# A diffusion backbone on one core: the first layer's modulation weights loaded by the features they make

## The reference, cut to what matters

```python
sh1, sc1, g1, sh2, sc2, g2 = split(silu(cvec) @ w_ada[l] + b_ada[l], 6)   # w_ada[l]: 1024 x 6144
hm = rmsnorm(x, norm_pre_mix[l]) * (1 + sc1) + sh1                        # modulate
rq, rk, rv, ... = split(hm @ w_in[l])                                     # first product
```

## Time and profile before

| | before |
|---|---|
| median of 3 runs | 2224.93 us (2220.21 to 2231.7) |
| the profiled execution, its own time | 2224.93 us |
| its span, first to last instruction | 2223.2 us |
| mean granted TensorE clock | 0.987 |
| TensorE busy | 2139.6 us, 96% |
| VectorE, ScalarE, GpSimd busy | 1562.2, 927.7, 112.7 us |

### The profile page before, as it was taken

How to read it: one execution, slowest core, us unless ns; L and a number is a source line. 1 busy time by engine, 2 the same in 40 slices (tenths; PEclk the granted TensorE clock), 3 DMA queues, 4 the chain that set the end, 5 groups by cost and what they waited for, 6 DMA issues and landing times. The chain is left out here.

```text
span 2223.2 us, 34106 instructions
## 1 busy us (share of the span) xinstructions
PE 2139.6 (96%) x14080; PEld 2029.8 (91%) x14080; DVE 1562.2 (70%) x2451; ACT 927.7 (42%) x1462; POOL 112.7 (5%) x208
## 2 busy tenths in 40 slices
PE   5999999999998999999979999999999989999997
PEld 3999999999978899999869999999999888999996
DVE  5677766477757787887776776755764557787785
ACT  4644432466243433333365454325653433333332
POOL 1000000110000000000000000111100000000000
PEclk9999999999999999999989999999999999999998
DMA  7333244234344222222323332542233411222223
GB/s 278 118 108 111 91 166 141 100 99 149 101 133 158 67 77 87 85 77 95 142 109 114 114 114 82 171 148 78 89 115 70 178 57 58 95 76 81 91 76 133
DMA packets 62955, 246.22 MB, mean 111 GB/s; under 512 B 8080, under 2 KB 8112, under 8 KB 60240
## 3 DMA queue, kind: packets, MB, share of 16 engines
q1 hardware_dynamic: 41040, 153.12, 20.9%
q0 software_dynamic: 21760, 90.91, 11.7%
HBM read 230.34 MB, written 13.66 MB: 110 GB/s over the span
## 5 line engine op out<-in xcount | busy, mean ns | idle before, releaser
L1499 DVE TENSOR_TENSOR wl<-raw,wh 128x1024 fp32r<-128x1024 f32 x204 | 247.1, 1222 | 148.7 <-ACT wh L1080 145.9
L476 PE MATMUL unit<-hmh,wh 128*128 128x320 f32 x1152 | 348.1, 310 | 2.9 <-DVE sig L1978 2.6
L477 PE MATMUL unit<-hml,wh 128*128 128x320 f32 x1152 | 347.4, 309 | 0.0
L1080 ACT ACTIVATE wh<-raw 128x1024 fp32r<-128x1024 f32 x204 | 210.0, 1050 | 128.1 <-DMA raw<-w_main 128.1
L479 PE MATMUL unit<-hmh,wl 128*128 128x320 f32 x1152 | 263.1, 310 | 0.0
L1599 DVE CUSTOM_DVE_ANT_0 junk<-ada,csb,par 128x1024 f32<-128x1024 f32 x160 | 205.6, 1285 | 29.1 <-DMA ada<-w_ada 9.0
L476 PEld LDWEIGHTS unit<-hmh,wh 128*128 128x128 f32 x1152 | 216.9, 188 | 4.1 <-issue 3.4
L477 PEld LDWEIGHTS unit<-hml,wh 128*128 128x128 f32 x1152 | 216.9, 188 | 0.7
L464 PE MATMUL unit<-wh,hmh 128*128 128x256 f32 (+1 forms) x640 | 201.6, 315 | 9.5 <-DVE t L1525 3.6
L466 PE MATMUL unit<-wh,hml 128*128 128x256 f32 (+1 forms) x640 | 199.8, 312 | 0.0
L465 PE MATMUL unit<-wl,hmh 128*128 128x256 f32 (+1 forms) x640 | 199.6, 312 | 0.0
(11 more groups left out here) (435 smaller groups left out, 5257.9 us busy)
## 6 DMA issues: line engine op xcount, KB each, us to landing
raw<-w_main SPq DMA_DIRECT2D x276, 512.0 KB, 4.1
ada<-w_ada POOLq DMA_DIRECT2D x80, 512.0 KB, 4.3
first<-w_first SPq DMA_DIRECT2D x8, 1024.0 KB, 19.3
x<-x_keep POOLq DMA_DIRECT2D x3, 2560.0 KB, 9.5
bias<-biases POOLq DMA_DIRECT2D x32, 192.0 KB, 2.7
x<-x POOLq DMA_DIRECT2D x2, 2560.0 KB, 12.4
x_keep<-x POOLq DMA_DIRECT2D x10, 512.0 KB, 2.9
bias<-biases POOLq DMA_DIRECT2D x16, 256.0 KB, 4.1
```

The costliest lines, as they stand in the source:

```text
L476: pe.matmul(u[:, h, 0:n], a[0], xs[h][0], start=f, stop=False)
L477: pe.matmul(u[:, h, 0:n], a[0], xs[h][1], start=False, stop=False)
L1080: act.activation(wh[slot[i]][:, :], raw[slot[i]][:, :], ACT.Copy).then_inc(w_hi[slot[i]], 1)
L1499: dve.tensor_tensor(wl[slot[i]][:, :], raw[slot[i]][:, :], f32(wh[slot[i]][:, :]), ALU.subtract)\
```

## The change

The first modulation weights are cut the other way: piece c now holds all 1024 input features of the 2 x 128 outputs (shift and scale) that modulate chunk c. TensorE's sums of one piece are 8 matmuls of 256 columns in four column groups (`first_sums`). The sums lie in rows 0 and 1 of each group of 32 rows, and one matmul with two columns of `zpos` (ones at the rows that are 0 or 1 modulo 32) both adds the four groups and turns them to columns (`turn_rows`). So that the other rows are zero, `cc` is padded to 32 columns. VectorE makes one chunk's shift and scale, modulates the chunk, and so on. On TensorE sums, turns and the products of the first two columns are interleaved in one loop. The tokens are loaded first, in three parts, on SyncE's queue; slabs 0 and 1 go ahead of piece 3. `x_back` counts one less, as the tokens have semaphores of their own.

```diff
-        zpos = fixed("zpos", [P, 2])
+        zpos = fixed("zpos", [P, 4])
-        cc = fixed("cc", [P, KD, 2])
+        cc = at("cc", [P, KD, 32], csb_at)
+        mrows = [at(f"mrows{i}", [P, 2 * P], csb_at + KD * 32 * 4 + i * 2 * P * 4) for i in range(2)]
-        wf = [at(f"first{k}", [P, 2 * D], k * 2 * D * 4) if k < 5 else u0(f"first{k}", [P, 2 * D]) for k in range(KD)]
-        mrows = u0("mrows", [P, 512])
+        wf = [at(f"first{c}", [P, KD, 2 * P], (2 - c) * B - KD * 2 * P * 4) if c < 2 else u0(f"first{c}", [P, KD, 2 * P]) for c in range(KD)]
...
 TensorE
-            pe.wait_ge(const_set, 1)
+            def first_sums(c):
+
+                pe.wait_ge(first_in[c], 16)
+                if c == 0:
+                    pe.wait_ge(tr_free, TILES)
+                    pe.wait_ge(zv_ready, halves_of(TILES - 1))
+                if c >= 2:
+                    pe.wait_ge(rows_ready, c - 1)
+                for k in range(KD):
+                    g = k % 4 * 32
+                    mm = pe.matmul(sc[c % 2][g:g + 32, 0:2 * P], cc[:, k, :], wf[c][:, k, :], start=k < 4, stop=k >= 4)
+                mm.then_inc(sums_ready, 1)
+
+            def turn_rows(c):
+
+                pe.wait_ge(rows_ready, c + 1)
+                if c >= 2:
+                    pe.wait_ge(first_mod, c - 1)
+                for a in range(2):
+                    mm = pe.matmul(tp[c % 2][:, 2 * a:2 * a + 2], mrows[c % 2][:, a * P:(a + 1) * P], zpos[:, 2:4], start=True, stop=True)
+                mm.then_inc(turned, 1)
+
+            pe.wait_ge(early_in, EARLY)
+            for _ in range(TILES):
+                turn_tile()
             pe.wait_ge(cc_ready, 1)
-            for k in range(KD):
-                pe.wait_ge(first_in[k], 16)
-                for n in range(4):
-                    mm = pe.matmul(unit[0][32 * n:32 * n + 2, 0, :], cc[:, k, :], wf[k][:, n * 512:(n + 1) * 512],
-                                   start=k == 0, stop=k == KD - 1)
-                if k == 4:
-                    pe.wait_ge(early_in, EARLY)
-                for _ in range((0, 0, 0, 0, 2, 2, 1, 0)[k]):
-                    turn_tile()
-            mm.then_inc(sums_ready, 1)
-            for half in range(2):
-                pe.wait_ge(rows_1, half + 1)
-                if half:
-                    pe.wait_ge(rows_2, 1)
-                for c in range(KD * half, KD * half + KD):
-                    rows = slice(c // 4 * 32, c // 4 * 32 + 2)
-                    mm = pe.transpose(unit[1 - half][:, c // 4 % 2, c % 4 * 2:c % 4 * 2 + 2], mrows[rows, c % 4 * P:(c % 4 + 1) * P], ident[rows, rows])
-            mm.then_inc(turned, 1)
-
-            def two_columns():
-
-                units = []
-                for _ in range(2):
-                    w, _, _ = slab(P)
-                    units.append((U.take(), w))
-                    U.add()
-                for k in range(KD):
+            units = []
+            for c in range(KD + 2):
+                if c < KD:
+                    first_sums(c)
+                if 1 <= c <= KD:
+                    turn_rows(c - 1)
+                if c == 2:
+                    for _ in range(2):
+                        w, _, _ = slab(P)
+                        units.append((U.take(), w))
+                        U.add()
+                if c >= 2:
+                    k = c - 2
                     pe.wait_ge(hm0_ready, k + 1)
                     for u, w in units:
                         for h in range(2):
                             mm = product(u[:, h, 0:HALF], w(k), [t[:, k, h * HALF:(h + 1) * HALF] for t in (hmh, hml)], k == 0, k == KD - 1)
                         if k == KD - 1:
                             mm.then_inc(unit_ready, 1)
...
 SyncE
             sp.dma_start(cc[:, :, :], ccol).then_inc(cv_load, 16)
-            for k in range(KD):
-                if k == KD - 1:
+            sp.dma_start(x[:, 0:1, :], x_in[:, 0:1, :]).then_inc(x_part[0], 16)
+            sp.dma_start(x[:, 1:3, :], x_in[:, 1:3, :]).then_inc(x_part[1], 16)
+            sp.dma_start(x[:, 3:TILES, :], x_in[:, 3:TILES, :]).then_inc(x_part[2], 16)
+            for c in range(KD):
+                if c == 3:
                     for i in range(2):
                         weights(i)
-                sp.dma_start(wf[k][:, :], w_first[k]).then_inc(first_in[k], 16)
+                sp.dma_start(wf[c][:, :, :], w_first[c]).then_inc(first_in[c], 16)
...
 GpSimd
             g.memset(epsc[:, :], EPS).then_inc(const_set, 1)
-            g.dma_start(x[:, :, :], x_in).then_inc(x_back, 16)
-            for to, of in ((lt[:, 5, :], decay), (ident[:, :], ident_in), (par[:, :, :], params), (zpos[:, :], zpos_in)):
+            for to, of in ((ident[:, :], ident_in), (lt[:, 5, :], decay), (par[:, :, :], params), (zpos[:, :], zpos_in)):
...
 ScalarE
-            act.wait_ge(x_back, 16)
             for t in range(TILES):
+                if t in (0, 1, 3):
+                    act.wait_ge(x_part[(t + 1) // 2], 16)
                 root(x[:, t, :], xu[:, t, :], ss2, rt2, t)
...
-            act.wait_ge(sums_ready, 1)
-            for n in range(3):
-                a = act.activation(mrows[32 * n:32 * n + 2, :], unit[0][32 * n:32 * n + 2, 0, :], ACT.Copy)
-                if n:
-                    a.then_inc(rows_1, 1)
-            for c in range(KD):
-                act.wait_ge(z_ready, c + 1)
-                act.activation(hmh[:, c, :], xt[:, c, :], ACT.Copy).then_inc(zh_ready, 1)
+            for c in range(KD + 1):
+                if c < KD:
+                    act.wait_ge(sums_ready, c + 1)
+                    if c >= 2:
+                        act.wait_ge(turned, c - 1)
+                    act.activation(mrows[c % 2][:, :], sc[c % 2][:, 0:2 * P], ACT.Copy).then_inc(rows_ready, 1)
+                if c >= 1:
+                    act.wait_ge(z_ready, c)
+                    act.activation(hmh[:, c - 1, :], xt[:, c - 1, :], ACT.Copy).then_inc(zh_ready, 1)
             split(2)
...
 VectorE
-            dve.wait_ge(sums_ready, 1)
-            dve.tensor_copy(mrows[96:98, :], unit[0][96:98, 0, :]).then_inc(rows_2, 1)
-            dve.wait_ge(turned, 1)
-            for half in range(2):
-                of = slice(half * KD, half * KD + KD)
-                dve.tensor_tensor(...)
-            scales_mix(0)
             dve.wait_ge(tr_free, TILES)
             for c in range(KD + 1):
                 if c < KD:
+                    both = slice(SH1 + c, SC1 + c + 1, KD)
+                    dve.wait_ge(turned, c + 1)
+                    dve.tensor_tensor(mod[:, 0, both, :], tp[c % 2][:, 0:4].rearrange("p (a n) -> p a n", a=2),
+                                      par[:, 0, B_ADA + SH1 + c:B_ADA + SC1 + c + 1:KD].unsqueeze(2).broadcast_to([P, 2, 2]), ALU.add)\
+                       .then_inc(first_mod, 1)
+                    dve.drain()
+                    dve.scalar_tensor_tensor(out=am1[:, 0, c, :], in0=mod[:, 0, SC1 + c, :], scalar=1.0,
+                                             in1=par[:, 0, N_PRE_MIX + c:N_PRE_MIX + c + 1].broadcast_to([P, 2]), op0=ALU.add, op1=ALU.mult)
+                    dve.drain()
                     for i, cols in STREAMS:
                         a = dve.tensor_scalar(xt[:, c, cols], xt[:, c, cols], am1[:, 0, c, i:i + 1], mod[:, 0, SH1 + c, i:i + 1],
                                               ALU.mult, ALU.add)
                     a.then_inc(z_ready, 1)
                 if c >= 1:
                     dve.wait_ge(zh_ready, c)
                     lo(hml[:, c - 1, :], xt[:, c - 1, :], hmh[:, c - 1, :]).then_inc(hm0_ready, 1)
```

More of the change, by code:

```diff
@@ L331, in build @@
         first_in = [sem(f"first_in{k}") for k in range(KD)]
-        cc_ready, sums_ready, rows_1, rows_2, turned = sems("cc_ready sums_ready rows_1 rows_2 turned")
+        x_part = [sem(f"x_part{t}") for t in range(3)]
+        cc_ready, sums_ready, rows_ready, turned, first_mod = sems("cc_ready sums_ready rows_ready turned first_mod")
         early_in, csb_in, zv_ready = sems("early_in csb_in zv_ready")
@@ L336, in build @@
         unit_free = [sem(f"unit_free{i}") for i in range(2)]
-        unit_hi, const_in, cv_load, const_set, ada_done, cs_ready, mod_ready = sems("unit_hi const_in cv_load const_set ada_done cs_ready mod_ready")
+        unit_hi, const_in, cv_load, const_set, ada_done, cs_ready = sems("unit_hi const_in cv_load const_set ada_done cs_ready")
         ss_ready, rt_ready, rr_ready, xn_ready, xs_ready = sems("ss_ready rt_ready rr_ready xn_ready xs_ready")
@@ L587, in two_columns @@
                             mm.then_inc(unit_ready, 1)
-                for n in range(2):
-                    slab_done.append((unit_ready, U.count - 1 + n))
+            for n in range(2):
+                slab_done.append((unit_ready, U.count - 1 + n))
             for l in range(DEPTH):
@@ L607, in _ @@
                             first_columns(2 * l - 1)
-                        else:
-                            two_columns()
```

(19 more changed lines are left out.)

## The result

The changed kernel takes 2254.8 us (median of 4 runs, 2252.07 to 2256.19) against 2224.99. The ratio on record, estimated from the single runs, is 1.0124, 95% interval 1.0102 to 1.0146 (the two medians alone give 1.0134). The forecast was 2250, in the range 2238 to 2260. In a second series on another occasion the same two kernels gave 2260.37 and 2226.73, a ratio of 1.0147 (1.0127 to 1.0168); that time lies 0.4 us above the range.

A forecast was written before the change was run, and what follows sets the result against it. TensorE was taken as the bound, each product waiting for a handover to VectorE and back. `values()` starts 23.4 us later, its low-clock start adds 1.6: +25 on 2224.93 gives 2250 us, range 2238 to 2260.

The forecast's parts named there:

- handover: In each loop round, TensorE waits from its turn through VectorE's modulation and low part until the product: 2.26 us.
- a round, clock high / low: One chunk's product, sums, turn and handover in TensorE's loop: 5.5 us at high clock, 7.95 us at low.
- a round, mixed: One loop round with half of the time at each clock level: 6.7 us, five full rounds 33.5 us.
- last short round: End of TensorE's loop, only a product, a turn and a handover: 4.5 us high, 6.1 low, 5.2 middle.
- L: End of VectorE's last low part in the loop: predicted at 74.1 us, against 50.72 in the kernel before.
- low start of `values()`: TensorE idles 3 to 5 us before `values()`, which so begins with the low clock: 1.6 us, ends 0 and 3.
- two idle stretches: TensorE, kernel before: 1.79 us idle before 634.00 was followed by clock 0.50, 2.33 us before 1113.87 was not.
- rival (b): Same chain in the loop, clock stays low: L 83.2, with the start +34 us, 2259 us; chance 0.12.
- rival (c): The handover is hidden, TensorE's own work decides in the loop: L 52.5, 2227 us, no change; chance 0.07.
- V: Start of `values()` on TensorE: predicted at 82.3 us, against 58.88 in the kernel before.
- Rival (d): Loading decides, the loop keeping pace with 2.5 us a chunk: L 38.3, `values()` at 46.5, 2212.5 us; chance 0.04.
- (a): Same chain in the loop, clock stays high: L 65.0, with the start about +16 us, 2241 us; chance 0.2.

The follow-up runs named there:

- the last kernel: lag 6 with decays and weight splits moved behind the tile copies but ahead of the loop; 2227.87 us, ratio 1.0014 to the kernel before.
- filled gaps: Changed kernel with twelve useless matmuls on TensorE between each turn and the wait of the product; 2248.19 us, ratio 1.0095 to the kernel before.
- lag 3: Changed kernel with TensorE's product of chunk c-3 instead of c-2 behind the turn of chunk c-1; 2232.49 us, ratio 1.004 to the kernel before.
- lag 6: Changed kernel with TensorE's product of chunk c-6 instead of c-2 behind the turn of chunk c-1; 2230.97 us, taken again 2230.69 us.

## Why the prediction was right

The mechanism was the one named, in the place named. The steps, predicted and measured:

| step | predicted | measured |
|---|---|---|
| first sums start | 26.9 | 27.32, behind ScalarE's copy |
| from there to the first product | 7.7 | 7.74 |
| idle in front of a product | 2.26 (handover) | 2.12 |
| a turn | 0.45 high, 0.6 low | 0.54 high (30.70 to 31.24), 0.94 low (30.53 to 31.47 in the last kernel), start to next start |
| a round, clock high / low | 5.5 / 7.95 | 5.68 high (filled gaps) |
| a round, mixed | 6.7 | 7.38 (five rounds, 35.06 to 71.94) |
| last short round | 5.2 | 5.78 |
| L | 74.1 | 78.56 |
| L to `values()` | 8.16 | 8.00 |
| low start of `values()` | 1.6 | 2.5 |
| whole | +25 us | +30 us |

The mis-sized term is the round with the mixed clock: 0.7 us in each of five rounds makes 3.4 of the 4.5 us by which L was late, the short round 0.6, the later start 0.4. The step that was wrong in it is the averaging. I took half of the *time* at each level, and that is near what the trace has: the mean clock of the five rounds is 0.66 to 0.76. But the 6.7 us is the mean of a whole high round and a whole low one, which puts half of the *work* at the low level, and the gap of 2.1 us does no work. If TensorE is at half speed for half of a round of R us, it loses a quarter of R, so R = 5.5 + R/4 = 7.3 us (7.6 with the measured 5.68); this is an estimate from these numbers, and 7.38 was measured. The low turn, too, was 0.94 us and not 0.6.

That half of the time was taken at all was a choice between two idle stretches that pointed in opposite directions, so that it came out near is partly luck. A single idle stretch in a busy surrounding is a poor guide to a loop that idles in every round. One sum was off by 0.1: the low end of the loop's start adds up to 27.3 us and not 27.4, by which rival (b) is 0.1 us late.

The experiments split the 27.8 us of L. Filling the gaps gives 10.4 (the low clock, 9.8 without the earlier start). From there to lag 3, 68.11 − 53.57 = 14.5 is the handover itself, as the seven gaps of 14.9 say. The last 2.9 us, 53.57 − 50.72, remain with lag 3, where no product waits for more than 0.65: what stands in front of the last low part is TensorE's own work in this order. That is rival (c), whose sum gave L 52.5 and +1.8 at V; measured with lag 3 it is +2.7. But it isn't the price of work that begins later: lag 6 starts its sums at 26.84 with the same work still to do, and has L 4.4 us and V 4.5 us earlier than the kernel before. There the sums and turns run ahead, VectorE gets its input sooner, and the products fill the end. Rival (d), the loading as the bound, is out: sums waited for no DMA in the loop. Rivals (a) and (b), a clock that stays at one level, did not occur.

The prediction charged a switch of TensorE between column groups and the full array with nothing. In the round at the high clock with filled gaps the turn starts 1.00 us behind the sums, with sums that span 1.07, and the sums start 0.24 behind the last matmul of a product, where matmuls are 0.15 apart:

```profile
41.75 0.31 PE L467 MATMUL unit<-hmh,wl 128*128 128x320 f32 x1
41.99 1.07 PE L564 MATMUL sc<-first,cc 128*32 128x256 f32 x16
42.99 0.61 PE L573 MATMUL tp<-zpos,mrows 128*128 128x2 f32 x4
```

So a switch shows as about 0.1 us, some 1.6 us for sixteen (an estimate from these starts). The Trainium skill, "TensorEngine Tiling (Array Packing)", section Tiling Modes, says that changing the tiling mode drains the engine; these starts don't contradict it, and the price is below the 2.7 us that the prediction worked out beside it.

What stays open: why the load near 1700 us takes 13 us in some executions and 17 in others, and why the median of lag 6, with its early start of `values()`, lies 5 us above the kernel before. The profiles place part of it (the step at 1700, and for one of them another between 540 and 663, both with a lower granted clock), but each shows one execution only. It isn't needed for the verdict on the change: the lag of the changed kernel is there by 130 us in both of its profiles (30.2 and 29.3). But the medians of the changed kernel and all its variants lie 2 to 11 us further behind than their V says. So the sizes of the single effects are read from the traces, one execution each, and the medians bear them out only to within that.

## What to carry to other kernels

In a pipeline written out by hand over two engines, follow each wait to the instruction that raises the semaphore, and then through everything that stands ahead of that instruction in its own engine's program. If the chain comes back to what the waiting engine issued last, the overlap is on paper only, and one stage more of distance or a swap of two steps removes most of it. Count the clock with it: here 2.1 us of idle time in each round of 7.2 cost another 1.5 us a round in slow matmuls, and a loop with useless work in the gap was faster than one with none. And let a mean of two levels say what it is a mean of: half of the time is not half of the work.

## What was not expected of the hardware

The granted clock went down and up once in nearly every round, in step with gaps of 2.12 us, and stayed up when they were 0.25 us. In the kernel before, a gap of 2.33 us passed without a fall, and the next one, of 2.32 us, was followed by a low stretch. Its row, and the window behind it (length, busy times, granted clock, DMA share, GB/s):

```profile
1122.83 1.97 PE L522 MATMUL sc<-ident,xs 128*128 128x128 f32 x8 [2.32 <-DVE xs L1539]
```
```profile
1122.83:1126.00 3.17, 3.17 (x12) 2.88 (x13) 3.08 (x3) 0.84 (x1) 0.00 (x0) 0.50 0.00 0
```

So in these two cases the length of the gap did not decide.
